# Front of a two-block kernel: modulation on TensorE in four column groups, all look-ups in one stretch, modulation tiles between the halves of a burst

## The chip, the core and the metric

One program runs on one core of a Trainium2 chip. The engines are TensorE (PE in the profile; its weight loads are PEld), VectorE (DVE), ScalarE (ACT), GpSimd (POOL), and SyncE (SP), whose queue issues the loads of weights. Each runs its own list of instructions in order and waits on semaphores. The metric is the time of one execution on the device, in microseconds (us), smaller is better.

## What is computed

Two blocks of a network on a sequence of 256 tokens and width 2048, in fp32. The change touches only the start of the first block:

```python
c_act = silu(c)
mod = c_act @ w_mod[l] + b_mod[l]                # (1, 2048) @ (2048, 6144)
shift, scale, gate = split(mod, 3)
h = rmsnorm(x, norm_gain[l]) * (1 + scale) + shift
proj = h @ w_in[l]                               # (256, 2048) @ (2048, 7248)
...
bias = rel_bias[t5_bucket(pos_q - pos_k)]        # table of 32 buckets x 8 heads
```

The rest (sparse attention, retention, output projection, a second layer, then a block with a convolution, a gated recurrence and a gated embedding) is computed as before.

## The kernel before

**Matmuls.** fp32 operands are split into a high and a low part: `w_hi` by ScalarE, `w_lo = raw - w_hi` by VectorE, and likewise `ht_hi`, `ht_lo` for the activations. A product is three matmuls (hi x hi, lo x hi, hi x lo), at L843 to L845 in the front and L684 to L686 in `gemm`. The output is made in chunks of 512 columns.

**The ring.** `raw` is a ring of four tiles of 1 MB (128 partitions x 4 x 512 fp32). SyncE loads tile t into place t % 4 when tile t-4 has been read. A tile of `w_in` holds four k-tiles of a chunk; it is split in two halves, each with a place in `w_hi` and `w_lo`, four places in all, which PE frees.

**The front** handles 40 tiles, in four rounds i = 0 to 3. Tiles 10i to 10i+7 are `w_mod`: the shift and scale columns of k-tiles 4i to 4i+3. Tiles 10i+8 and 10i+9 are the rows of `w_in` for these k-tiles, for the first two chunks. In a round:

- `modulate` (L2075, L2078), VectorE: multiplies each tile by the column of silu(c) and adds it up in `macc`, two instructions a tile; then one addition of the two halves (L2105).
- `pair_sums` (L816), PE: eight fp32 matmuls with a column of ones sum `macc` over the partitions, which puts shift and scale into columns.
- `columns` (L2062, L2065), VectorE: adds `b_mod`, and forms the scale with `norm_gain`.
- `turn_rows` (L828), PE, and `turned_rows` (L1377), ScalarE: transposes of the scaled rows of x.
- `formed_tiles` (L1393, L1395), ScalarE, and `tiles_low` (L2086), VectorE: apply scale and shift and split the result.
- `quarter_half(i, g, h)` (L843 to L845), PE: twelve matmuls with half h of the `w_in` tile of chunk g; four of them are the burst of a round.

**The look-ups** of the position bias, 24 steps, run between all this. A step: PE spreads the bucket numbers over partitions (`spread_keys`, L778, bf16); ScalarE makes a one-hot matrix by Abs and Relu (L1368, L1370, fp32); PE multiplies it with the table `rb_diag` (`look_up`, L790, four fp32 matmuls of 32 columns). Every four steps ScalarE copies the result to `bias` (`bias_out`). `STEPS` spreads the steps: four before round 0, one or two around each quarter of rounds 0 to 2.

PE runs an fp32 matmul as two instructions, so the trace counts eight for four.

## Time and profile before

| | |
|---|---|
| median of three runs | 1871.63 us (1869.8 to 1871.9) |
| the profiled execution | 1869.93 us, its span 1868.1 us |
| PE busy | 1826.4 us, 98% |
| VectorE, ScalarE busy | 1351.8 and 990.8 us, 72% and 53% |
| DMA, mean of the span | 227 GB/s |

The span is the time from the first to the last instruction of the profiled execution; the rest of its time lies around it. A matmul's end in the profile is modelled and overlaps the next, so the distance of starts is what a matmul costs. "Releaser" is the event that ended a wait.

### The profile page before, as it was taken

The page shows a single profiled execution, that of the slowest core. Times are in us where ns is not written, and L with a number is a line of the kernel's source. Part 1 is how long each engine was busy: PE and PEld are TensorE (multiplying, and loading weights), DVE is VectorE, ACT ScalarE, POOL GpSimd, SP SyncE. Part 2 cuts the span into 40 slices and gives each one's busy share as a digit, 9 for nine tenths or more (in the row PEclk, how much of TensorE's full clock was granted, in tenths as well). Part 3 has the DMA queues.
Part 4 walks back from the last instruction along what each step waited for, and adds up shares of the span by engine and source line. Part 5 has one row for each costly group of instructions (what it writes and reads, how often), then busy time and mean ns, then how long its engine had stood idle before and what let it go on. Part 6 is the DMA issues. An engine that isn't in the chain of part 4 may idle for free.

```text
span 1868.1 us, 25006 instructions
## 1 busy us (share of the span) xinstructions
PE 1826.4 (98%) x9520; PEld 1512.4 (81%) x9520; DVE 1351.8 (72%) x1949; ACT 990.8 (53%) x1359; POOL 203.0 (11%) x256
## 2 busy tenths in 40 slices
PE   5989999999999999999999999999999999999997
PEld 3768788889888878888888888888888888888886
DVE  6979999988987778857765544488885466665555
ACT  6664455446447445544654644476765445444464
POOL 0000002100000000210000000044441020031001
PEclk9989999999999999999999999999999999999999
DMA  9989978965986986744365555554555555557562
GB/s 350 373 323 343 332 232 302 322 224 182 330 297 229 361 280 225 235 159 159 124 225 185 182 199 192 191 181 161 177 178 182 185 191 184 184 180 248 182 197 94
DMA packets 211826, 424.07 MB, mean 227 GB/s; under 512 B 7680, under 2 KB 12684, under 8 KB 210316
## 3 DMA queue, kind: packets, MB, share of 16 engines
q1 hardware_dynamic: 209788, 414.94, 65.6%
q10 hardware_dynamic: 1936, 7.76, 1.0%
q8 instruction: 66, 1.08, 0.2%
q14 instruction: 36, 0.29, 0.0%
HBM read 418.45 MB, written 4.21 MB: 226 GB/s over the span
## 4 chain that ended last, share of the span: by engine, by line
PE 91%; DMA 3%; DVE 2%; ACT 2%; issue 1%; SPq 0%; DVEq 0%; POOLq 0%; POOL 0%; ACTq 0%
PE acc L684 28%; PE acc L686 28%; PE acc L685 28%; DMA raw<-in_w_in 2%; DVE scr L2078 1%; DMA raw<-in_w_mod 1%; PE tps L725 1%; PE tps L765 1%; ACT w_hi L1418 0%; ACT proj L1393 0%; PE sps L996 0%; PE tps L988 0%; PE sps L952 0%; PE sps L893 0%; PE sps L892 0%
## 5 line engine op out<-in xcount | busy, mean ns | idle before, releaser
L1859 DVE TENSOR_TENSOR w_lo<-raw,w_hi 128x1024 fp32r<-128x1024 f32 (+1 forms) x580 | 721.1, 1249 | 444.8 <-ACT w_hi L1246 442.5
L1246 ACT ACTIVATE w_hi<-raw 128x1024 fp32r<-128x1024 f32 (+1 forms) x580 | 606.1, 1050 | 762.3 <-PE acc L686 684.3
L684 PE MATMUL acc<-w_hi,ht_hi 128*128 128x512 f32 (+1 forms) x2304 | 910.5, 395 | 0.5 <-issue 0.4
L686 PE MATMUL acc<-w_hi,ht_lo 128*128 128x512 f32 (+1 forms) x2304 | 894.2, 388 | 0.0
L685 PE MATMUL acc<-w_lo,ht_hi 128*128 128x512 f32 (+1 forms) x2304 | 892.3, 387 | 0.0
L686 PEld LDWEIGHTS acc<-w_hi,ht_lo 128*128 128x128 f32 x2304 | 432.4, 188 | 90.3
L684 PEld LDWEIGHTS acc<-w_hi,ht_hi 128*128 128x128 f32 x2304 | 432.9, 188 | 87.4 <-issue 3.2
L685 PEld LDWEIGHTS acc<-w_lo,ht_hi 128*128 128x128 f32 x2304 | 433.3, 188 | 83.4
L1989 DVE SCALAR_TENSOR_TENSOR scr<-raw,vcol,scr 128x512 f32<-128x512 f32 x154 | 110.9, 761 | 4.8 <-issue 0.4
L2078 DVE SCALAR_TENSOR_TENSOR scr<-raw,vcol,scr 128x1024 f32<-128x1024 f32 x56 | 68.0, 1278 | 6.6 <-DMA raw<-in_w_mod 6.6
L1989 DVE SCALAR_TENSOR_TENSOR proj<-raw,vcol,proj 128x512 f32<-128x512 f32 x70 | 52.3, 788 | 1.9
L2684 POOL TENSOR_TENSOR scr<-scr 128x128 f32<-128x128 f32 x56 | 31.0, 586 | 157.0 <-DVE scr L2433 157.0
L2621 POOL COPY xn<-proj 128x128 f32<-128x128 f32 x4 | 2.5, 652 | 330.8 <-ACT proj L1483 330.8
L2655 POOL TENSOR_TENSOR proj<-proj 128x512 f32<-128x512 f32 x8 | 13.4, 1688 | 223.9 <-ACT proj L1602 192.8
L843 PE MATMUL acc<-w_hi,ht_hi 128*128 128x512 f32 x64 | 29.7, 465 | 7.2 <-DVE ht_lo L2086 7.2
L790 PEld LDWEIGHTS sps<-proj 128*128 128x128 f32 x192 | 28.9, 230 | 6.8 <-ACT proj L1370 4.2
L790 PE MATMUL sps<-proj 128*128 128x32 f32 x192 | 30.3, 307 | 3.3 <-ACT scr L1357 1.6
L1466 ACT ACTIVATE proj<-acc,st 128x512 f32<-128x512 f32 (+1 forms) x50 | 31.4, 679 | 0.1
L2646 POOL TENSOR_TENSOR scr<-scr,proj 128x384 f32<-128x384 f32 x16 | 23.2, 1447 | 56.2 <-DVE st L2248 56.2
L2720 POOL TENSOR_TENSOR xn<-proj 128x256 f32 x16 | 19.5, 1236 | 79.3 <-DVE proj L2528 48.6
L1483 ACT ACTIVATE proj<-acc 128x1024 f32<-128x1024 f32 (+1 forms) x26 | 25.7, 988 | 4.4 <-PE acc L845 4.3
L844 PE MATMUL acc<-w_lo,ht_hi 128*128 128x512 f32 x64 | 27.8, 434 | 0.0
(305 smaller groups left out, 1446.8 us busy)
## 6 DMA issues: line engine op xcount, KB each, us to landing
raw<-in_w_in SPq DMA_DIRECT2D x208, 1024.0 KB, 5.1
raw<-in_w_mod SPq DMA_DIRECT2D x64, 1024.0 KB, 6.2
raw<-in_w_mod SPq DMA_DIRECT2D x64, 512.0 KB, 6.3
raw<-in_w_out SPq DMA_DIRECT2D x32, 1024.0 KB, 5.2
raw<-in_w_o SPq DMA_DIRECT2D x16, 1024.0 KB, 5.2
raw<-in_w_ple_gate SPq DMA_DIRECT2D x16, 1024.0 KB, 5.1
raw<-in_w_b_out SPq DMA_DIRECT2D x8, 1024.0 KB, 5.1
raw<-in_w_a_out SPq DMA_DIRECT2D x8, 1024.0 KB, 5.1
```

The lines of the kernel that those rows point to most:

```text
L684: pe.matmul(o, hi_m, w_hi[:, slot, u, 0:width], start=start, stop=False)
L685: pe.matmul(o, hi_m, w_lo[:, slot, u, 0:width], start=False, stop=False)
L686: mm = pe.matmul(o, lo_m, w_hi[:, slot, u, 0:width], start=False, stop=stop)
L790: mm = pe.matmul(bias_cols[:, c:c + KPG * NH], onehot[:, n % 2, e * w + m * P:e * w + (m + 1) * P], rb_diag, start=True, stop=True)
L843: pe.matmul(o, hi_m, w_hi[:, slot, u, :], start=kt == 0, stop=False)
L844: pe.matmul(o, hi_m, w_lo[:, slot, u, :], start=False, stop=False)
L1246: act.activation(w_hi[:, x % SPL, :, 0:width], raw[:, j, 2 * (x % halves):2 * (x % halves) + 2, 0:width], ACT.Copy).then_inc(hi_ready, 1)
L1466: r = act.activation(o[:, m, :], acc[:, b, m, :], func, scale=st[:, 22 + m:23 + m])
L1859: dve.tensor_tensor(w_lo[:, x % SPL, :, 0:width], raw[:, j, 2 * (x % halves):2 * (x % halves) + 2, 0:width], w_hi[:, x % SPL, :, 0:width]. ...
L1989: r = dve.scalar_tensor_tensor(to[:, e, :], raw[:, slot, 2 * u + e, :], v2("c", kt), to[:, e, :], ALU.mult, ALU.add)
L2078: r = dve.scalar_tensor_tensor(to, src, v2("c", kt), to, ALU.mult, ALU.add)
L2684: pool.tensor_tensor(first_half[0], mid, first_half[1], ALU.subtract)
```

## The change

Four things change in the front, and nothing behind it.

1. *Modulation on PE.* `mod_slot(i, j)` multiplies tile 10i+j: four fp32 matmuls of 512 columns. The stationary operand is a column of silu(c) repeated 32 times, so each matmul fills one group of 32 columns of the array and writes 32 partitions of one bank of PSUM (`tps`, half 1): k-tile parity and shift or scale give the group. VectorE copies the bank after the eighth tile (`rows_out`), and `pair_sums` becomes four matmuls of two columns with `picks`, which adds the two parities. The ring place of a `w_mod` tile is freed by PE (`mod_read`); SyncE's waits are counted by `slot_free(t)`.
2. *Look-ups in one stretch.* All 24 come before round 0's burst, with tiles 1 to 7 of round 0 between them (`MOD_AFTER`). The one-hot is one VectorE comparison to bf16; `rb_diag` is split into three bf16 parts by GpSimd, so a step has 12 bf16 matmuls. Key columns go through four banks of `acc`, results through two of `sps`.
3. *Slots between halves of a burst.* Tiles 0 and 1 of round i+1 come after the first quarter of burst i, 2 and 3 after the second, 4 to 7 after the third; then come `turn_rows`, `pair_sums` of round i+1, the fourth quarter, and the second `turn_rows`.
4. *ScalarE's order* follows: a round is `w_hi`, `formed_tiles`, `w_hi`, `formed_tiles`, `w_hi` twice, then `scaled_rows` and both `turned_rows` of the next round.

```diff
-FIRST_STEPS = 4
-STEPS = [(0, 1, (1, 1, 2, 1)), (1, 1, (1, 1, 2, 1)), (1, 1, (1, 1, 2, 1)), (0, 0, (0, 0, 0, 0))]
+MOD_AFTER = {0: 1, 2: 2, 6: 3, 9: 4, 12: 5, 16: 6, 20: 7}
...
+            def slot_free(t):
+
+                i, j = divmod(t - RAW, 10)
+                if t < RAW:
+                    return
+                if j < 8:
+                    sp.wait_ge(mod_read, 8 * i + j + 1)
+                else:
+                    sp.wait_ge(raw_read, 8 + 4 * i + 2 * (j - 7))
...
-                        mm = pe.matmul(bias_cols[:, c:c + KPG * NH], onehot[:, n % 2, e * w + m * P:e * w + (m + 1) * P],
-                                       rb_diag, start=True, stop=True)
+                        for b in range(3):
+                            mm = pe.matmul(bias_cols(n)[:, c:c + KPG * NH], onehot[:, n % 4, e * w + m * P:e * w + (m + 1) * P],
+                                           rb_parts[:, b, :], start=b == 0, stop=b == 2)
...
+            def mod_slot(i, j):
+
+                t = 10 * i + j
+                if j == 0:
+                    pe.wait_ge(mod_taken, 1 + 2 * i)
+                pe.wait_ge(raw_landed[t % RAW], landed_start(t))
+                for u in range(2):
+                    c_col = v2("c", 2 * j + u).broadcast_to([P, 32])
+                    for b in range(2):
+                        g = 32 * (2 * b + u)
+                        mm = pe.matmul(tps[g:g + 32, 1, :], c_col, raw[:, t % RAW, 2 * u + b, :], start=j == 0, stop=j == 7)
+                mm.then_inc(mod_read, 1)
...
-            for i, (a, b, inside) in enumerate(STEPS):
-                pair_sums()
-                steps(n, a + b)
-                n += a + b
-                lo.skip(16)
-                for q, (g, h) in enumerate(((0, 0), (0, 1), (1, 0), (1, 1))):
-                    quarter_half(i, g, h)
-                    steps(n, inside[q])
-                    n += inside[q]
-                    if i < 3 and q < 2:
-                        turn_rows(4 * (i + 1) + 2 * q)
+            pair_sums()
+            for i in range(4):
+                for q in range(4):
+                    quarter_half(i, q // 2, q % 2)
+                    if i < 3 and q < 3:
+                        mod_slots(i + 1, 2 * q, 4 if q == 2 else 2)
+                        if q == 2:
+                            turn_rows(4 * (i + 1))
+                            pair_sums()
+                if i < 3:
+                    turn_rows(4 * (i + 1) + 2)
...
             for i in range(4):
                 for g in range(2):
                     t = 10 * i + 8 + g
...
                         act.activation(w_hi[:, 2 * g + h, :, :], raw[:, t % RAW, 2 * h:2 * h + 2, :], ACT.Copy)\
                            .then_inc(hi_ready, 1)
+                        if g == 0:
+                            formed_tiles(4 * i + 2 * h)
+                if i < 2:
+                    scaled_rows(i + 2)
                 if i < 3:
+                    turned_rows(4 * (i + 1))
+                    turned_rows(4 * (i + 1) + 2)
...
+            def rows_out(i):
+
+                dve.wait_ge(mod_summed, m_free.next(2))
+                dve.wait_ge(mod_read, 8 * (i + 1))
+                dve.tensor_copy(mrows, tps[:, 1, :]).then_inc(mod_ready, 1)
...
+            for j in range(24):
+                dve.wait_ge(keys_spread, j + 1)
+                if j >= 4:
+                    dve.wait_ge(onehot_used, j - 3)
+                dve.tensor_scalar(onehot[:, j % 4, :], key_cols(j), kst[:, C_NB:C_NB + 1], 0.0, ALU.add, ALU.is_equal)\
+                   .then_inc(onehot_ready, 1)
```

On PE, in the program of before, the end of burst 0 and the sums of round 1 stand like this (L778 and L790 are a look-up step; the burst's repeated rows are left out at "..."):

```order
L843 MATMUL acc<-w_hi,ht_hi 128x512
L844 MATMUL acc<-w_lo,ht_hi 128x512
L845 MATMUL acc<-w_hi,ht_lo 128x512
L778 MATMUL sps<-proj 128x256 x2
L790 MATMUL sps<-proj 128x32 x4
L816 MATMUL tps<-kst,scr 128x1 x8
```

and in the changed program, from the third quarter of burst 0 on (L846 is `mod_slot`, L870 `turn_rows`, L859 `pair_sums`, L885 to L887 the quarters):

```order
L887 MATMUL acc<-w_hi,ht_lo 128x512
L846 MATMUL tps<-raw,vcol 32x512 x16
L870 MATMUL tps<-kst,proj 128x128 x4
L859 MATMUL tps<-kst,scr 128x2 x4
L885 MATMUL acc<-w_hi,ht_hi 128x512
...
L887 MATMUL acc<-w_hi,ht_lo 128x512
L870 MATMUL tps<-kst,proj 128x128 x4
```

Tiles 4 to 7 of the next round (16 matmuls) and its sums now stand ahead of the fourth quarter, and the second group of transposes behind it; in before the whole burst stood ahead of the next sums, and the transposes between its quarters.

On ScalarE in the changed program, from the `w_hi` of chunk 1 in round 0 to the first ones of round 1 (L1454 is `w_hi`, L1420 `scaled_rows`, L1413 `turned_rows`, L1428 and L1430 `formed_tiles`), with what each waits for:

```order
L1454 ACTIVATE w_hi<-raw 128x1024 [waits split_used]
L1420 ACTIVATE proj<-xres,st 128x512 x2
L1413 ACTIVATE proj<-tps 128x512 [waits xt_turned] x2
L1454 ACTIVATE w_hi<-raw 128x1024 [waits split_used,raw_landed2]
L1428 ACTIVATE proj<-proj,modc,acol 128x256 [waits columns_ready]
L1428 ACTIVATE proj<-proj,modc,acol 128x256
L1430 ACTIVATE ht_hi<-proj 128x512 [waits tiles_formed]
L1454 ACTIVATE w_hi<-raw 128x1024 [waits split_used]
```

Both transposed row tiles of the next round are copied ahead of its first `w_hi`, and forming stands between the two halves of a `w_in` tile. In before the copies stood between look-up steps, and the two `w_hi` of a tile side by side:

```order
L1377 ACTIVATE proj<-tps 128x512 [waits xt_turned]
L1368 ACTIVATE proj<-sps,kst 128x512 [waits onehot_used,keys_spread]
L1370 ACTIVATE proj<-proj,kst 128x512 [waits spread_read]
...
L1418 ACTIVATE w_hi<-raw 128x1024 [waits split_used,raw_landed2]
L1418 ACTIVATE w_hi<-raw 128x1024 [waits split_used]
```

On VectorE the start of the front is now, all look-ups ahead of round 0 (L2120 the comparison, L2104 the row copy, L2134 `w_lo`, L2110 `ht_lo`):

```order
L2120 TENSOR_SCALAR proj<-acc,kst 128x512 x16
L2000 TENSOR_TENSOR proj<-vcol 128x8
L2104 COPY scr<-tps 128x512
L2094 TENSOR_TENSOR modc<-tps,vcol 128x2x4
L2097 SCALAR_TENSOR_TENSOR acol<-modc,vcol 128x4
L2134 TENSOR_TENSOR w_lo<-raw,w_hi 128x1024
```

The 64 products of `modulate` that stood there and in every round are gone.

## Rows read from the trace of the kernel before

**Rows 1.** The page's chain that ended last, shares of the span by engine.
```profile
PE 91%; DMA 3%; DVE 2%; ACT 2%; issue 1%; SPq 0%; DVEq 0%; POOLq 0%; POOL 0%; ACTq 0%
```

**Rows 2.** Stretches: length; PE, PEld, DVE, ACT, POOL busy; PEclk, DMA share, GB/s.
```profile
20.00:50.00 30.00, 21.60 (x85) 17.71 (x86) 26.02 (x28) 23.49 (x42) 0.00 (x0) 1.00 1.05 387
80.00:110.00 30.00, 27.38 (x167) 22.99 (x167) 27.22 (x27) 20.30 (x32) 0.00 (x0) 0.89 1.01 366
```

**Rows 3.** Chain of waits in order of time: start, length, what.
```profile
31.42 8.48 DMA raw<-in_w_in
...
116.44 8.63 DMA raw<-in_w_in
...
130.38 0.79 PE acc L843
```

**Rows 4.** Timeline: start, length, instruction, [idle before, releaser]; third and last burst.
```profile
118.73 0.48 PE L843 MATMUL acc<-w_hi,ht_hi 128*128 128x512 f32 x1
...
119.30 2.48 DVE L2078 SCALAR_TENSOR_TENSOR scr<-raw,vcol,scr 128x1024 f32<-128x1024 f32 x2 [0.49 <-DMA raw<-in_w_mod]
...
121.33 0.39 PE L845 MATMUL acc<-w_hi,ht_lo 128*128 128x512 f32 x1
...
123.19 1.92 PE L816 MATMUL tps<-kst,scr 128*128 128x1 f32 x16 [0.65 <-DVE scr L2105]
...
130.97 0.63 PE L844 MATMUL acc<-w_lo,ht_hi 128*128 128x512 f32 x1
...
133.51 0.40 PE L844 MATMUL acc<-w_lo,ht_hi 128*128 128x512 f32 x1
```

**Rows 5.** Groups by line, 0 to 143 us: busy, mean ns | idle before, releaser.
```profile
L2078 DVE SCALAR_TENSOR_TENSOR scr<-raw,vcol,scr 128x1024 f32<-128x1024 f32 x56 | 68.0, 1278 | 6.6 <-DMA raw<-in_w_mod 6.6
...
L790 PEld LDWEIGHTS sps<-proj 128*128 128x128 f32 x192 | 28.9, 230 | 6.8 <-ACT proj L1370 4.2 <-ACT scr L1357 2.4
...
L2113 DVE TENSOR_TENSOR w_lo<-raw,w_hi 128x1024 fp32r<-128x1024 f32 x16 | 19.2, 1222 | 3.2 <-ACT w_hi L1418 3.1
L1370 ACT ACTIVATE proj<-proj,kst 128x512 f32<-128x512 f32 x24 | 17.4, 723 | 0.8
...
L1418 ACT ACTIVATE w_hi<-raw 128x1024 fp32r<-128x1024 f32 x16 | 16.0, 1047 | 8.5 <-DMA raw<-in_w_in 8.5
...
L1393 ACT ACTIVATE proj<-proj,modc,acol 128x256 f32<-128x256 f32 x16 | 8.6, 588 | 0.6 <-DVE acol L2065 0.6
...
L1395 ACT ACTIVATE ht_hi<-proj 128x512 fp32r<-128x512 f32 x8 | 5.0, 630 | 0.7
...
L1377 ACT ACTIVATE proj<-tps 128x512 f32<-128x512 f32 x8 | 4.8, 598 | 19.4 <-PE tps L828 19.4
...
L778 PEld LDWEIGHTS sps<-proj 128*128 128x128 bf16 x64 | 4.2, 106 | 12.9 <-ACT proj L1368 8.4 <-issue 3.1 <-DVE proj L1963 1.1
```

**Rows 6.** Timeline of PE at fp32 matmuls elsewhere in the kernel.
```profile
297.62 0.60 PE L952 MATMUL sps<-proj,scr 128*128 128x256 f32 x2
298.05 0.38 PE L951 MATMUL sps<-proj,scr 128*128 128x128 f32 x2
...
1247.41 0.73 PE L1078 MATMUL sps<-scr 128*32 128x32 f32 x62
...
1247.96 0.20 PE L1078 MATMUL sps<-scr 128*32 128x32 f32 x1
```

**Rows 7.** Timeline: first spread, one fp32 look-up, four transposes.
```profile
17.70 0.61 PE L778 MATMUL sps<-proj 128*128 128x256 bf16 x2 [0.73 <-DVE proj L1963]
...
43.85 1.92 PE L790 MATMUL sps<-proj 128*128 128x32 f32 x8 [0.69 <-ACT scr L1357]
...
52.65 0.64 PE L828 MATMUL tps<-kst,proj 128*128 128x128 f32 x4
```

**Rows 8.** Groups by line and shape on DVE: a read of 384 PSUM columns.
```profile
L1963 DVE SCALAR_TENSOR_TENSOR proj<-sps,proj 128x384 bf16<-128x384 f32 x1 | 0.6, 558 | 2.7 <-PE sps L797 2.7
```

**Rows 9.** The page's DMA issues: count, size, us from issue to landing.
```profile
raw<-in_w_in SPq DMA_DIRECT2D x208, 1024.0 KB, 5.1
```

More of the change, by code:

```diff
@@ L69 @@
 C_PW = C_HPI + 1
-C_TH = C_PW + 2
+C_SEL = C_PW + 2
+C_TH = C_SEL + 2
 C_N = C_TH + NB - EXACT - 1
@@ L528, in _ @@
             free = Seen(sp, raw_read)
+            def slot_free(t):
[6 more added lines that the diff above has]
+                    sp.wait_ge(raw_read, 8 + 4 * i + 2 * (j - 7))
             def mod_pair(i, j):
                 slot = (10 * i + j) % RAW
-                sp.wait_ge(raw_read, free.next(2))
+                slot_free(10 * i + j)
                 for b in range(2):
@@ L570, in _ @@
                 for g in range(2):
-                    land((10 * i + 8 + g) % RAW, full(wi[0])(i, CHUNKS[g] * CH, CH))
+                    slot_free(10 * i + 8 + g)
+                    slot = (10 * i + 8 + g) % RAW
+                    sp.dma_start(raw[:, slot, :, :], full(wi[0])(i, CHUNKS[g] * CH, CH)).then_inc(raw_landed[slot], 16)
+            free.skip(16)
             for l in range(DEPTH):
@@ L777, in spread_keys @@
                     at = P * (g0 + e)
-                    mm = pe.matmul(key_cols[:, e * w:(e + 1) * w], key_pick[:, at:at + P], b_t, start=True, stop=True)
+                    mm = pe.matmul(key_cols(n)[:, e * w:(e + 1) * w], key_pick[:, at:at + P], b_t, start=True, stop=True)
                 mm.then_inc(keys_spread, 1)
             def look_up(n):
-                if n % 4 == 0 and n:
-                    pe.wait_ge(bias_ready, n // 4)
+                if n % 4 == 0 and n >= 8:
+                    pe.wait_ge(bias_ready, n // 4 - 1)
                 pe.wait_ge(onehot_ready, n + 1)
@@ L799, in _, with mod_slots @@
             pe.wait_ge(buckets_ready, 1)
-            pe.wait_ge(s_rb, 16 * KPG)
+            pe.wait_ge(rb_split, 1)
             spread_keys(0)
-            def steps(n, count):
-                for j in range(n, n + count):
-                    if j < 23:
-                        spread_keys(j + 1)
-                    look_up(j)
+            spread_keys(1)
+            pe.wait_ge(vec_ready, 1)
+            def mod_slot(i, j):
[9 more added lines that the diff above has]
+                mm.then_inc(mod_read, 1)
+            def mod_slots(i, first, count):
+                if i < 4:
+                    for j in range(first, first + count):
+                        mod_slot(i, j)
             def pair_sums():
-                pe.wait_ge(mod_taken, m_taken.next())
-                m_taken.skip(1)
+                m_taken.skip(2)
                 pe.wait_ge(mod_ready, m_ready.next())
-                for b in range(2):
-                    for j in range(4):
-                        mm = pe.matmul(tps[:, 1, 4 * b + j:4 * b + j + 1], macc[:, b, 0, j * P:(j + 1) * P], ones,
-                                       start=True, stop=True)
+                for j in range(4):
+                    mm = pe.matmul(tps[:, 1, 2 * j:2 * j + 2], mrows[:, j * P:(j + 1) * P], picks, start=True, stop=True)
                 mm.then_inc(mod_summed, 2)
@@ L1360, in bias_out @@
                 r.then_inc(bias_ready, 1)
-            def steps(n, count):
-                for j in range(n, n + count):
-                    o = onehot[:, j % 2, :]
-                    act.wait_ge(keys_spread, j + 1)
-                    if j >= 2:
-                        act.wait_ge(onehot_used, j - 1)
-                    act.activation(o, key_cols, ACT.Abs, bias=kst[:, C_NB:C_NB + 1]).then_inc(spread_read, 1)
-                    act.wait_ge(spread_read, j + 1)
-                    act.activation(o, o, ACT.Relu, bias=ones, scale=-1.0).then_inc(onehot_ready, 1)
-                    if j % 4 == 0 and j:
-                        bias_out(j // 4 - 1)
             def turned_rows(k):
@@ L1406, in _ @@
             act.activation(vcol[:, P + KT:P + NV2], tps[:, 0, P + KT:P + NV2], ACT.Copy).then_inc(vec_ready, 1)
+            bias_out(3)
             turned_rows(0)
+            bias_out(4)
+            scaled_rows(1)
             turned_rows(2)
-            for i, (a, b, inside) in enumerate(STEPS):
+            bias_out(5)
+            for i in range(4):
                 for g in range(2):
                     t = 10 * i + 8 + g
-                    if g:
-                        steps(n, a)
                     for h in range(2):
@@ L2115, in _ @@
                         own.skip(1)
-                for e in range(2):
-                    if i < 3:
-                        if e == 0:
-                            dve.wait_ge(mod_summed, m_free.next(2))
-                        modulate(i + 1, 0, e)
-                    tiles_low(4 * i + 2 * e)
+                        if g == 0:
+                            tiles_low(4 * i + 2 * h)
             results.skip(16)
```

136 lines of the change are left out of this document (64 added, 72 removed).

## The prediction

> **What bounds the kernel now.** I read the chain that ended last first. Its line by engine [rows 1] gives 91% of the span to the matrix engine (PE), so a change that neither removes matmul time nor moves a stretch in which PE waits can do nothing. The table by stretches [rows 2] then says where PE waits: in the front the DMA engines are busy at 1.01 to 1.05 of their time and move 366 to 387 GB/s, while PE has holes, and its granted clock averages 0.89 from 80 to 110 us. The chain of waits in time [rows 3] joins the two: tiles of `w_in` land at 39.90 and 125.07 us (start plus length of the DMA rows), ScalarE and VectorE split the last and form `ht`, and at 130.38 PE starts the last round's burst of matmuls for the first two chunks. From there the chain is PE's. So the front is a stream of 40 tiles of 1 MB, and everything behind it is PE's. What moves the start at 130.38 moves the end by as much, and only that counts here.
>
> How fast can the stream go? At 387 GB/s a tile of 1.049 MB takes 2.71 us; call it 2.7. From tile 9 (39.90) to tile 39 (125.07) 30 tiles took 85.2 us, which is 81.0 at that rate and 4.2 us lost. Tile 37, the last of `w_mod`, landed at 119.30 [rows 4], where VectorE's wait for it ends. Hence a perfect stream gains about 4 us, 0.2%, and that is the ceiling of this change unless it shortens what comes behind the last tile.
>
> **What the change removes.** On VectorE the 56 multiply-adds of 1.28 us and 8 first products [rows 5], and on ScalarE an Abs and a Relu for each of 24 look-ups, the Relu 0.72 us [rows 5]. Neither engine ends the front except where it holds a tile of the ring of four. In before a `w_mod` tile is held for 2.5 us, within the 2.7 of the next transfer. So the removal is hidden under the DMA, and would come out on the path only as part of those 4.2 us.
>
> **What PE gets.** A tile of `w_mod` is now four fp32 matmuls over 512 columns. The trace shows fp32 over 256 columns as two instructions in 0.43 us (297.62 to the next at 298.05) [rows 6], so 512 columns cost 0.86 us at the higher clock and 1.7 at the lower. Do the four 32-column groups run at once? The nearest row is 62 fp32 instructions of 32x32 into different groups, whose starts fill 0.73 less one duration of 0.20, 0.53 us, 8.6 ns each [rows 6], where 32 of 256 columns' worth would be 27 ns: three at a time. I take 0.9 to 1.0 us a tile. The page "TensorE: Matmul & The Clock Gate" of the Trainium skill (Part 3) has a measured 2.38x for three column groups over 512 columns; by that a tile would be about 1.1 us by estimate, and the sum would grow by some 0.2 us a round.
>
> A look-up step keeps its two bf16 spreads and has 12 bf16 matmuls of 32 columns for 8 fp32 instructions. The latter took 1.92 us at the lower clock [rows 7] and are paced by their weight loads, 230 ns mean; bf16 loads are 106 ns [rows 5]. So 12 cost between 0.4 and 1.3 us at the lower clock; I take 0.6, with 0.43 for the spreads: 1.0 a step, 0.5 at the higher clock. VectorE's comparison reads 512 columns of PSUM: 384 took 0.56 [rows 8], so in proportion at most 0.74 and not under 0.56; I take 0.69, or 0.75 with the hand-off. VectorE sets the pace of a step where the clock is high, PE where it is low.
>
> **First stretch.** Look-ups start as before at 17.70 [rows 7]. 24 steps of 0.75 are 18 us, and seven tiles of 0.9 between them 6.3: about 42 us. Before, two thirds of the look-ups lay later, under the DMA stream. What is queued behind them now? ScalarE issues all six copies of the bias before the first `w_hi`, and VectorE all 24 comparisons before the first row copy. So tile 8, which landed in before at 37.2 (2.7 ahead of tile 9), waits: row copy 0.65, sums 0.96, forming 1.81, second `w_hi` 1.05, second `w_lo` 1.22 (all priced below), hand-offs and two small operations 0.9 give 48.6 us for its release. A transfer on an idle queue takes 5.1 us from issue to landing [rows 9], 2.4 more than its 2.7, so tile 12 flows from 51.0. The stream, if full, is done with tile 11 at 39.90 + 2 x 2.7 = 45.3. Idle 5.7 us.
>
> **Rounds 1 and 2.** This is the term on which the forecast rests, and the order of instructions shows it. PE's burst of round i is stretched over the whole round: its fourth quarter comes only after the eighth modulation tile and the sums of round i+1. ScalarE must turn the last two row tiles, which PE transposes after that quarter, before it may touch the first `w_in` tile of round i+1, although that tile landed long ago. The tile's place in the ring is thus late. Counted from the landing of the last `w_mod` tile, at the higher clock: PE multiplies it, 1.0; VectorE copies rows, 0.65; sums, half of the 16 instructions in 1.92 us [rows 4], 0.96; a quarter, 12 matmuls, eleven starts in 2.60 us [rows 4], 2.8; transposes 0.64 [rows 7]; ScalarE's copy 0.60, `w_hi` 1.05, forming 1.81 (two of 0.59 and one of 0.63), `w_hi` 1.05; VectorE's `w_lo` 1.22 [rows 5]; hand-offs 0.7. That is 12.5 us, and with 2.4 to the first byte 14.9. Four tiles, the rest of the ring, cover 10.8. Idle 4.1 us. The second `w_in` tile is released 4.0 us after the first (forming and two `w_hi` more), the transfer covers 2.7: 1.3 more. Each such round loses 5.4 us.
>
> In before the burst of a round ran beside the multiply-adds: the fourth quarter of round 2 had its last matmul at 121.33, two us behind the landing of tile 37 [rows 4], so nothing held the first `w_in` tile.
>
> **The sum.** Losses: first stretch 5.7 + 1.3 = 7.0; two rounds (tiles 22 and 32) 10.8; together 17.8 us. If all of the 4.2 us lost in before disappear, tile 37 is 13.6 us later, if none 17.8; I take the middle, 15.7. Behind tile 37 the way to PE's last burst is the same chain up to forming, 1.0 + 0.65 + 0.96 + 2.8 + 0.64 + 0.60 + 1.05 + 1.81 + 0.7 + 0.6 = 10.8 us, against 130.38 - 119.30 = 11.1 before. No term. The profiled execution took 1869.9 us (span 1868.1 and 1.8 around it), 1.7 below the median of the three runs: 1869.9 + 15.7 = 1885.6, on the median's scale 1887.
>
> **The rivals.**
> *The clock stays low.* In before the last burst begins with matmuls 0.63 us long, at 130.97, and has 0.40 at 133.51 [rows 4], the lower and the higher level; a stretch of the front averages 0.89 [rows 2]. If PE keeps the lower level (1.2 GHz of 2.4) in the look-ups, 24 steps of 1.0 and eight tiles of 1.8 take 38.4 instead of 24 us, 14 more; in each of two rounds the tile, the sums, a quarter and the transposes cost 0.85 + 0.95 + 2.4 + 0.4, 4.6 more. Up to 23 us on top, 1910; half of it 1899. For it: new rounds have a tile of 1 us and then 1.7 of nothing. Against: tiles are dense matmuls and the first stretch is full of work. By "TensorE: Matmul & The Clock Gate" of the Trainium skill, a DMA wait between all matmuls makes PE run cold; the trace agrees in that its clock fell where PE waited. Chance 0.26.
> *The groups don't run together.* With the two instructions of a matmul blocking the next group, 1.7 us a tile: 7 us in the first stretch, 0.9 a round, about 1896; all serial, 3.4 us a tile exceeds the transfer, and eight tiles and a burst of 11 make a round of 40 us against 27, over 1930. Against it are [rows 6]. 0.07.
> *Faster: the ring never runs dry.* If the chain of 12.5 us is under 8.4 (10.8 less 2.4), the stream is full, tile 37 lands at 39.90 + 28 x 2.7 = 115.5 instead of 119.30, and the time is 3.8 us lower, 1868. It is decided at the release of the first `w_in` tile of a round. The first stretch would have to be done by 35 us too, which VectorE's 18 us alone from 17.70 nearly forbid. 0.09.
> *No difference*: half of the chain is shorter than I count and the 4.2 us come back against the rest. 0.05; a loss of 4 to 8 us, 0.03.
> My case has 0.50, with a range of its own of 1881 to 1894.
>
> **The numbers.** A measurement here tells 0.2%, 3.7 us, from no change. Faster 0.09, same 0.05, slower 0.86. The range leaves out the faster case and the top of the low-clock and serial cases: 1873 to 1909.
>
> **What would show it.** Right: in the changed profile DMA share under 0.9 in three places, about 46 to 51, and twice some 30 us later each; rounds of about 32 us where they are 28 now (30 tiles in 85.2); ScalarE's first `w_hi` of a round waiting for PE's transposes, not for a landing; PE's last burst of the front starting at about 146. The modulation tile at 0.9 to 1.0 us, starts of four groups together. Wrong: first `w_hi` right after a landing and DMA share above 1.0 to the end of the front (faster), or 0.43 us a matmul in most bursts (slower still). A look-up step far from 0.75 us moves the first term alone.

## The result: 1.1% slower

| | before | changed |
|---|---|---|
| median | 1870.72 us (1868.33 to 1871.9, 4 runs) | 1890.49 us (1886.81 to 1893.64, 4 runs) |
| ratio | | 1.0107 (95%: 1.0084 to 1.0129) |
| profiled execution, its span | 1869.93, 1868.1 us | 1886.81, 1884.7 us |
| last burst of the front starts | 130.38 | 147.03 |
| VectorE, ScalarE busy | 1351.8, 990.8 us | 1294.4, 959.3 us |

The forecast was 1887 with a range from 1873 to 1909. VectorE and ScalarE are relieved of 57 and 32 us of work, and the program is 20 us slower. In the profiled executions all of the difference, 16.6 us of span, is there when the last burst begins (147.03 - 130.38 = 16.65).

### The profile page after: what moved, and what is told of

Same layout as the page of the kernel before. It is cut to its first block, busy times and chain, and to the rows that moved or that the text cites. A ratio compares the mean times of both kernels' runs of the same rounds, so it can differ in the third digit from the quotient of the medians.

```text
span 1884.7 us, 25534 instructions
## 1 busy us (share of the span) xinstructions
PE 1838.9 (98%) x9840; PEld 1496.3 (79%) x9840; DVE 1294.4 (69%) x1909; ACT 959.3 (51%) x1311; POOL 203.9 (11%) x261
## 4 chain that ended last, share of the span: by engine, by line
PE 95%; DMA 2%; DVE 1%; ACT 1%; issue 1%; SPq 0%; ACTq 0%; DVEq 0%; POOLq 0%; POOL 0%
PE acc L714 28%; PE acc L716 27%; PE acc L715 27%; DMA raw<-in_w_mod 2%; PE tps L846 1%; PE tps L755 1%; PE acc L885 1%; PE acc L886 1%; PE tps L795 1%; PE acc L887 1%; PE sps L828 0%; PE sps L941 0%; PE acc L808 0%; PE sps L1044 0%; PE tps L1036 0%
## 5 line engine op out<-in xcount | busy, mean ns | idle before, releaser
L714 PEld LDWEIGHTS acc<-w_hi,ht_hi 128*128 128x128 f32 x2304 | 432.8, 188 | 87.4 <-issue 2.9
L846 PE MATMUL tps<-raw,vcol 128*32 128x512 f32 x256 | 36.7, 662 | 9.9 <-DMA raw<-in_w_mod 9.9
L885 PE MATMUL acc<-w_hi,ht_hi 128*128 128x512 f32 x64 | 30.3, 473 | 15.5 <-DVE ht_lo L2110 15.5
L1413 ACT ACTIVATE proj<-tps 128x512 f32<-128x512 f32 x8 | 4.8, 597 | 76.4 <-PE tps L870 76.4
L2104 DVE COPY scr<-tps 128x512 f32<-128x512 f32 x4 | 2.8, 690 | 54.8 <-PE tps L846 54.8
L885 PEld LDWEIGHTS acc<-w_hi,ht_hi 128*128 128x128 f32 x64 | 14.2, 222 | 24.2 <-DVE ht_lo L2110 16.3
L2134 DVE TENSOR_TENSOR w_lo<-raw,w_hi 128x1024 fp32r<-128x1024 f32 x16 | 19.2, 1224 | 16.3 <-ACT w_hi L1454 16.2
```

What stands on the lines that cost most here:

```text
L714: pe.matmul(o, hi_m, w_hi[:, slot, u, 0:width], start=start, stop=False)
L846: mm = pe.matmul(tps[g:g + 32, 1, :], c_col, raw[:, t % RAW, 2 * u + b, :], start=j == 0, stop=j == 7)
L885: pe.matmul(o, hi_m, w_hi[:, slot, u, :], start=kt == 0, stop=False)
```

## The profile after

The chain of the changed kernel by engine, and stretches of it (start:end, length, busy us and instructions of PE, PEld, DVE, ACT and POOL, then PEclk, DMA share, GB/s). They answer to [rows 1] and [rows 2]:

```profile
PE 95%; DMA 2%; DVE 1%; ACT 1%; issue 1%; SPq 0%; ACTq 0%; DVEq 0%; POOLq 0%; POOL 0%
```

```profile
20.00:50.00 30.00, 26.59 (x434) 18.10 (x431) 20.90 (x33) 18.05 (x37) 0.00 (x0) 0.93 0.88 313
44.00:54.00 10.00, 7.39 (x28) 4.24 (x28) 6.17 (x6) 7.35 (x11) 0.00 (x0) 0.66 0.54 173
54.00:76.00 22.00, 17.00 (x104) 9.37 (x100) 1.02 (x3) 1.96 (x3) 0.00 (x0) 1.00 1.04 383
76.00:88.00 12.00, 9.28 (x40) 5.79 (x40) 6.20 (x6) 7.46 (x12) 0.00 (x0) 0.86 0.69 230
80.00:110.00 30.00, 23.67 (x125) 12.43 (x123) 4.91 (x8) 6.57 (x10) 0.00 (x0) 0.89 0.97 347
88.00:108.00 20.00, 15.67 (x89) 7.70 (x88) 1.02 (x3) 0.93 (x2) 0.00 (x0) 0.91 1.05 388
108.00:122.00 14.00, 10.24 (x44) 6.39 (x44) 6.20 (x6) 7.27 (x11) 0.00 (x0) 0.76 0.67 221
```

A full stream has a DMA share of 1.04 to 1.05 here and moves 383 to 388 GB/s. The shares of 0.54, 0.69 and 0.67 mark three holes, one a round; between them the stream is full. How long a hole is I read from the landings, as the forecast did: a tile is late by what it lands more than 2.7 us behind its predecessor. Tiles 12 and 13 are 5.3 us late together, 22 and 23 4.9, 32 and 33 6.1, 16.4 us in all. The bytes in the rows above say the same (387 - 173 of 387 GB/s over 10 us is 5.5, then 4.9 and 6.0); the share of busy time alone would give 4.9, 4.1 and 5.1, which is too little. VectorE, busy for 27 of 30 us in [rows 2], now works for 1.0 us in the 20 from 88 to 108: what the change set free had not bounded these rounds. (The PEclk of 1.00 in the first line of [rows 2] is not the level of the first burst of before: its matmuls start 0.43 us apart from 46.34 us on, the lower level, as they do in the changed kernel from 46.61.)

Why the hole opens is in the chain of waits of round 1 (start, length, what; the quarter's twelve matmuls are cut to two):

```profile
59.53 8.71 DMA raw<-in_w_mod
...
68.28 1.11 PE tps L846 x8
...
69.48 0.70 DVE scr L2104
...
70.23 1.05 PE tps L859 x8
71.29 0.34 PE acc L885
...
73.93 0.23 PE acc L887
74.16 0.45 PE tps L870 x4
...
75.13 1.05 ACT w_hi L1454
76.17 0.99 ACT proj L1428 x2
```

Tile 17, the last of `w_mod`, lands at 68.24. The `w_in` tile behind it lands at 70.95 and is then left alone: ScalarE takes it up at 75.13, when PE has gone through the tile, the sums, a whole quarter and the transposes. VectorE's second `w_lo` from it ends at 80.08, and only then may the place be loaded again.

The last round, in the timeline:

```profile
133.50 1.94 PE L846 MATMUL tps<-raw,vcol 128*32 128x512 f32 x8 [0.79 <-DMA raw<-in_w_mod]
135.36 1.12 PE L870 MATMUL tps<-kst,proj 128*128 128x128 f32 x4
...
136.31 1.87 PE L859 MATMUL tps<-kst,scr 128*128 128x2 f32 x8
...
139.04 0.63 PE L887 MATMUL acc<-w_hi,ht_lo 128*128 128x512 f32 x1
...
142.94 0.60 ACT L1413 ACTIVATE proj<-tps 128x512 f32<-128x512 f32 x1 [5.83 <-PE tps L870]
143.43 1.05 ACT L1454 ACTIVATE w_hi<-raw 128x1024 fp32r<-128x1024 f32 x1
...
147.03 0.50 PE L885 MATMUL acc<-w_hi,ht_hi 128*128 128x512 f32 x1 [4.13 <-DVE ht_lo L2110]
```

Here PE runs at its lower level: the row of the tile is 1.94 us long where it was 1.11 at 68.28, the matmuls of the quarter start 0.43 us apart and not 0.23. From the start of tile 7's multiplication to the first matmul of the burst it is 10.44 us in round 1 (78.72 - 68.28) and 13.53 in the last.

## The experiments

All are edits of the changed kernel and compute what it computes. A tile is "late" by what it lands more than 2.7 us behind its predecessor; the middle columns add this up for the two tiles that follow each pair of `w_in` tiles in the ring. The last two columns are the start of the last burst and how long that is after the landing of tile 37, the last of `w_mod`. All but the ratio are of the one profiled execution.

| run | ratio to before (95%) | 12, 13 late | 22, 23 late | 32, 33 late | last burst at | behind tile 37 |
|---|---|---|---|---|---|---|
| before | 1 | 0 | 0 | 0 | 130.4 | 11.1 |
| the changed kernel | 1.0107 (1.0084 to 1.0129) | 5.3 | 4.9 | 6.1 | 147.0 | 13.6 |
| early_turn | 1.0054 (1.0040 to 1.0068) | 7.3 | 4.8 | 3.0 | 140.8 | 7.7 |
| slots_two | 1.0015 (1.0006 to 1.0024) | 6.0 | 2.8 | 1.0 | 133.6 | 6.3 |
| late_look | 1.0098 (1.0082 to 1.0113) | 4.1 | 8.6 | 9.1 | 154.6 | 13.5 |
| both | 1.0022 (1.0013 to 1.0031) | 3.3 | 4.7 | 2.0 | 135.2 | 6.3 |
| warm | 1.0090 (1.0074 to 1.0107) | 6.5 | 7.5 | 6.0 | 150.3 | 11.7 |
| warm_few | 1.0080 (1.0066 to 1.0094) | 6.5 | 5.6 | 4.2 | 146.1 | 10.5 |
| two_groups | 1.0134 (1.0117 to 1.0151) | 6.1 | 5.7 | 5.7 | 153.5 | 11.3 |
| whole_burst | 1.0155 (1.0138 to 1.0172) | 6.6 | 2.6 | 2.5 | 159.4 | 7.9 |
| hi_first | 1.0009 (1.0000 to 1.0018) | 3.0 | 0 | 0.7 | 131.5 | 7.3 |
| tuned | 0.9987 (0.9978 to 0.9996) | 1.5 | 0.9 | 0 | 129.2 | 7.3 |
| after_again (no edit) | 1.0111 (1.0094 to 1.0128) | 5.4 | 8.6 | 10.5 | 155.1 | 14.4 |

**early_turn: the second transposes ahead of the fourth quarter.**

```diff
                             pair_sums()
-                if i < 3:
-                    turn_rows(4 * (i + 1) + 2)
+                            turn_rows(4 * (i + 1) + 2)
```

> The changed kernel with the second group of row transposes of the next round moved on TensorE from behind the fourth quarter to ahead of it. Order theory (ScalarE's first w_hi of a round waits for the copy of these transposes, and they for the quarter): in the changed kernel's profile the quarter takes 2.85 us at 71.15 and ScalarE's w_hi starts at 75.13; it should start some 2.8 us earlier, the idle time of the DMA stream ahead of tiles 22 and 32 should fall from 3.7 and 4.5 us to about 1 and 1.5, and the last burst, which starts at 147.03, should start about 9 us earlier, near 138: some 9 us less than the changed kernel, 1.006 of before (now 1.0107). Clock theory (what is lost comes from TensorE at its lower level): the order of two small groups changes no clock, so under 2 us less. First-stretch theory (the 5 us lost ahead of tile 12 are most of it and the rest is fixed): under 3 us less.

Half of the loss went with one moved line: 1.0107 to 1.0054, 9.9 us by the ratios. In round 1 ScalarE's `w_hi` now starts at 75.54 for a tile taken up at 70.46, 5.1 us behind, where it was 6.85 (75.13 - 68.28), although PE was at its lower level:

```profile
75.05 0.60 ACT L1412 ACTIVATE proj<-tps 128x512 f32<-128x512 f32 x1 [0.97 <-PE tps L870]
75.54 1.05 ACT L1453 ACTIVATE w_hi<-raw 128x1024 fp32r<-128x1024 f32 x1
```

The lateness of tiles 22 and 32 fell from 3.7 and 4.6 us to 2.6 and 0.4, that of 23 and 33 rose from 1.2 and 1.6 to 2.2 and 2.6: the second `w_in` tile, behind both formings, is the next limit. The last burst started at 140.8 and not at the forecast 138, 6.3 us earlier than in the changed kernel, and 5.9 of these 6.3 us lie behind tile 37 (7.7 us for 13.6), where the changed kernel also ran at the lower level, which cost it 3.1 us (above). So the order is worth some 2.8 us there. In rounds 1 and 2 the holes fell from 11.0 to 7.8 us together, but the first stretch, which the edit does not touch, lost 2.0 us more in this execution. How the 9.9 us divide between order and clock this run does not tell.

**slots_two: two modulation tiles behind every quarter.**

```diff
-                    if i < 3 and q < 3:
-                        mod_slots(i + 1, 2 * q, 4 if q == 2 else 2)
-                        if q == 2:
-                            turn_rows(4 * (i + 1))
-                            pair_sums()
+                    if i < 3:
+                        mod_slots(i + 1, 2 * q, 2)
+                        if q in (1, 2):
+                            turn_rows(4 * (i + 1) + 2 * (q - 1))
                 if i < 3:
-                    turn_rows(4 * (i + 1) + 2)
+                    pair_sums()
```

> The changed kernel with two modulation tiles behind each of the four quarters in place of two, two, four and none, both groups of row transposes behind the second and third quarter, and the sums last. Order theory: no quarter stands any more between the last w_mod tile and the first w_hi. From that landing the chain is tile 1.0, row copy 0.7, sums 1.0, two small operations 0.4, forming, w_hi and w_lo, about 7.8 us to the release of the first w_in tile, under the 8.4 (four tiles of 2.7 less 2.4) that a full stream allows. Idle ahead of tiles 22 and 32 about 0, ahead of 23 and 33 about 0.6: 9 to 10 us less up to tile 37 (133.5 in the changed kernel), and 5 to 6 less behind it, since the last burst then starts 7.5 us behind tile 37 and not 13.5. Last burst near 131.5, time about that of before, 0.999 to 1.002 of it. Clock theory: the waits for tiles are as long as before, the clock falls as often, and no more than 5 us come back, 1.008. First-stretch theory: under 3 us.

1.0015, 17 us less than the changed kernel; the first `w_hi` of a round waits for its own transfer:

```profile
65.57 0.60 ACT L1412 ACTIVATE proj<-tps 128x512 f32<-128x512 f32 x1 [4.83 <-PE tps L870]
72.00 1.06 ACT L1453 ACTIVATE w_hi<-raw 128x1024 fp32r<-128x1024 f32 x1 [5.83 <-DMA raw<-in_w_in]
```

```profile
44.00:54.00 10.00, 6.83 (x32) 4.13 (x32) 6.53 (x8) 8.17 (x12) 0.00 (x0) 0.83 0.56 183
...
76.00:88.00 12.00, 10.98 (x48) 6.22 (x47) 4.01 (x4) 4.44 (x7) 0.00 (x0) 0.78 0.96 335
...
108.00:122.00 14.00, 13.26 (x79) 6.93 (x82) 2.38 (x3) 1.72 (x3) 0.00 (x0) 0.98 0.94 337
```

The second and third hole shrink to 2.8 and 1.0 us, while the first, which the edit doesn't touch, stays (6.0 us, 5.3 before the edit). The clock fell here too (0.78 from 76 to 88), so it cannot be the main cause of what was lost. The last burst, forecast near 131.5, starts at 133.6.

**late_look and both: eight look-ups moved into round 0.** In `late_look` 16 look-ups stand first; the others follow one by one behind quarters and tiles of round 0, with their columns in the two banks of `sps`. `both` has this and `slots_two`.

```diff
+            def look_on(i, n):
+                if i == 0:
+                    look_up(n)
+                    if n < 23:
+                        spread_keys(n + 1)
...
```

> The changed kernel with 16 look-ups ahead of the first burst and the last eight one by one behind quarters and modulation tiles of round 0 (keys and results in the two banks of sps, as in before). Order theory with its first term: the first stretch ends some 6 us earlier, the release of tile 8 with it, so that the idle time of 4.3 us ahead of tile 12 and 1.0 ahead of tile 13 goes; the later rounds keep theirs (3.7 and 4.5 us). Last burst 147.0 less 5 = 142, time 5 us less, 1.008 of before. If the look-ups are not what holds tile 8 (the clock or the sums do), 0 to 1 us less. If eight steps in the round delay the modulation tiles, up to 3 us come back.

> The two edits together (two modulation tiles behind each quarter, and 16 look-ups first with eight in round 0). Order theory: the stream is never dry; tile 37 lands at 38 + 29 x 2.7 = about 117.5 to 118 with small losses, the last burst starts 7.5 behind it, at 125 to 126, where before has 130.38: 4 to 5 us faster than before, 0.9975. If the two gains overlap, or a low clock is the cost, 1.000 to 1.005.

Neither came as expected. `late_look` is not told from the changed kernel (1.0098, intervals overlap), `both` not from `slots_two`. The first burst did start earlier, at 43.8 and 44.4 where it was 46.6 and 47.4. But the look-ups were not gone, only moved into a round that has no room on PE. In `both`, from 50 to 72 us:

```profile
50.00:72.00 22.00, 21.79 (x232) 12.46 (x224) 5.50 (x9) 2.96 (x5) 0.00 (x0) 0.99 0.97 349
```

```profile
69.34 1.06 PE L851 MATMUL tps<-raw,vcol 128*32 128x512 f32 x8
69.44 0.75 DVE L2139 TENSOR_SCALAR proj<-sps,kst 128x512 bf16<-128x512 f32 x1 [2.98 <-PE sps L813]
70.33 0.47 PE L826 MATMUL sps<-proj 128*128 128x32 bf16 x12
...
70.73 1.06 PE L851 MATMUL tps<-raw,vcol 128*32 128x512 f32 x8
```

PE is busy for 21.8 of 22 us, and no tile of the round's end (L851) waits for a transfer: tile 17 landed at 67.17 and is multiplied at 70.73, so PE is late. In `late_look` tiles 12 and 13 are 1.2 us less late than in the changed kernel, but tile 17 is 1.5 us late itself and lands at 68.60, where it was 68.24: what the shorter first stretch won was gone by then. The larger holes behind it cannot be put down to the edit. The profiled execution of `late_look` was the slowest of its four (1894.4 us, two others 1886.2 and 1886.5), all three of its fourth quarters ran at the lower level, and `after_again`, without any edit, shows holes as large. My forecast had priced the first stretch, not what its work costs elsewhere.

**warm and warm_few: TensorE kept busy in its waits.** bf16 matmuls that nothing reads, eight (`warm`) or three (`warm_few`) behind each of the tiles 4 to 6, and sixteen behind the last transposes of a round. As they write the banks that held the look-ups' results, the first burst also waits for the last copy of the bias (`bias_ready`) in both runs; it started no later for it (46.6 and 46.1).

```diff
+            def fill(n):
+                for k in range(n):
+                    pe.matmul(sps[:, k % 2, 0:384], ident_b, key_pick[:, 0:384], start=True, stop=True)
...
```

> The changed kernel with work added that nothing reads: eight bf16 matmuls of 384 columns behind each of the modulation tiles 4, 5 and 6 of a round, and sixteen behind the last transposes of a round, into the two banks of sps, free by then. They fill TensorE's waits for transfers and for the forming. Clock theory (rival of the forecast): if waiting is what lets the granted clock fall, these stretches stay at the higher level, tiles at 133.5 take 1.0 and not 1.94, the quarter behind them 2.85 and not 4.3, the last burst's first 8 matmuls 0.23 and not 0.43 each: about 4 to 6 us less than the changed kernel, 1.008 of before. Order theory alone: these low stretches are a cost of 1 us in a round and 2.5 at the end, so 3 to 4 us less at most, and the DMA stream stays idle ahead of tiles 22 and 32. If the added matmuls only lengthen the chain: 0 to 3 us more.

> The changed kernel with three added matmuls of 384 columns behind the modulation tiles 4, 5 and 6 in place of the eight of the run warm (sixteen behind the last transposes as there). In warm the clock stayed at the higher level from the fourth quarter to the last burst, and from the start of tile 7's multiplication to the burst it was 10.45 us against 13.5 in the last round of the changed kernel, but the eight matmuls kept tile 7 waiting for some 2 us a round. Clock theory: with 0.6 us of filling the tile is not late, and the clock stays high where the filling is: 3 to 6 us less than the changed kernel, 1.008 of before. If three are too few to keep the clock: like the changed kernel, 1.0105.

With three, the last round of the front reads:

```profile
135.64 1.06 PE L846 MATMUL tps<-raw,vcol 128*32 128x512 f32 x8 [1.72 <-DMA raw<-in_w_mod]
...
137.59 1.05 PE L868 MATMUL tps<-kst,scr 128*128 128x2 f32 x8 [0.29 <-DVE scr L2115]
...
141.81 2.77 PE L852 MATMUL sps<-proj 128*128 128x384 bf16 x16
146.11 0.50 PE L894 MATMUL acc<-w_hi,ht_hi 128*128 128x512 f32 x1 [1.54 <-DVE ht_lo L2121]
```

```profile
134.00:138.00 4.00, 2.07 (x16) 0.99 (x16) 0.69 (x1) 0.60 (x1) 0.00 (x0) 1.00 1.05 386
138.00:142.00 4.00, 4.00 (x24) 3.40 (x24) 0.33 (x2) 0.00 (x0) 0.00 (x0) 1.00 1.05 387
142.00:146.00 4.00, 2.57 (x16) 1.98 (x14) 1.86 (x2) 3.90 (x6) 0.00 (x0) 1.00 0.50 185
146.00:150.00 4.00, 3.89 (x17) 3.23 (x18) 3.07 (x4) 3.89 (x7) 0.00 (x0) 1.00 0.29 75
```

The clock is 1.00 to the burst and through it, and tile to burst takes 10.47 us again, so the 13.53 of the changed kernel are 10.5 of work and 3.1 of lower clock. The time is 5.0 us under that of the changed kernel (1.0080 for 1.0107; 1.0111 in its second comparison, below), with intervals that just overlap. Three quarters of the loss stayed, so the clock is the smaller part of it. The 5.0 us are net: what the fillers themselves cost is in them too. With eight the clock was 1.00 from the fourth quarter to the last burst as well (the third quarters, from 94.05 and 128.06, still ran 0.43 us apart), and the time was 1.0090, not told from the changed kernel: at 139.88 tile 37 was multiplied 1.2 us after it had landed (138.7), because the fillers stood ahead of it.

**two_groups: four column groups against two.**

```diff
-                        g = 32 * (2 * b + u)
+                        g = 32 * (2 * b + j % 2)
```

(with `start` for the first and `stop` for the last matmul of each group).

> The changed kernel with the four matmuls of a modulation tile in two column groups (the tile's parity picks which two of the four, so the sums are the same) and not in four. In the changed kernel a tile takes 0.99 us at the higher clock where four matmuls one by one would be 3.4. If the overlap comes from the groups, a tile takes 1.75 us, 0.75 more; the first stretch holds eight of them between the look-ups (5 to 6 us longer), a round's chain one (0.8, twice, and once at the end): 7 to 8 us more than the changed kernel, 1.015 of before. If the matmuls overlap whatever group they are in, or the tile is hidden by the transfers everywhere: 0 to 1 us more.

```profile
75.61 1.91 PE L846 MATMUL tps<-raw,vcol 128*32 128x512 f32 x8 [0.80 <-DMA raw<-in_w_mod]
77.45 0.66 PE L871 MATMUL tps<-kst,proj 128*128 128x128 f32 x4
```

A tile takes 1.84 us (77.45 - 75.61) with two groups and 1.00 with four (69.28, where the transposes start, less 68.28), at the same clock. The overlap comes from the groups, and is nearly complete: four matmuls one by one would be 3.4. The time is 1.0134, 5.0 us more than the changed kernel by the ratios, with intervals that overlap. The profile is clearer: with eight such tiles ahead of it the first burst starts at 53.9, and in the two executions of the changed kernel at 46.6 and 46.2.

**whole_burst: no slots inside a burst.** Four quarters in a row, then the transposes, the eight tiles, the sums.

> The changed kernel with the slots taken out of the burst: four quarters in a row, then both groups of transposes, then the eight modulation tiles and the sums. Order theory: the quarter is no longer in the chain behind the last w_mod tile (5 us less per round there, 5 to 6 at the end), but the next round's first two tiles wait for 11 us of burst in the ring in place of 5, so that some 5 us of the stream are lost at the ring's other end in each of three rounds. About even with the changed kernel: 5 less to 5 more, 1.008 to 1.013. If slots inside the burst are themselves what costs (more waits, a lower clock): 8 us less or better. If the ring is what matters and the fourth quarter is not: 10 to 15 more.

1.0155, 9.0 us more than the changed kernel, so more than the 5 that I gave as the most, and short of the 10 to 15 for "the ring is what matters":

```profile
54.00:76.00 22.00, 16.48 (x91) 7.13 (x89) 0.00 (x0) 1.19 (x2) 0.00 (x0) 0.81 0.69 243
...
88.00:108.00 20.00, 16.05 (x89) 9.49 (x88) 1.73 (x2) 2.71 (x5) 0.00 (x0) 0.93 0.61 209
```

The ring fills with `w_mod` while PE is in the burst: tiles 14, 24 and 34 are late by 7.2, 7.7 and 8.1 us, new idle time at another place. Where the quarter has left the chain, the holes do shrink (2.6 and 2.5 us for 4.9 and 6.1), as does the way behind tile 37 (7.9 us, at the lower level). So the slots themselves are right; what costs is the quarter that is left behind the last of them.

**hi_first and tuned: the order mended at both ends.** `hi_first` is `slots_two` with ScalarE in the order of `w_hi` twice, forming, `w_hi` twice, forming. `tuned` also splits tile 8 ahead of the second row copy and the last bias copy, tile 9 ahead of the forming, and has PE multiply tiles 0 and 1 of round 1 ahead of the first burst; its look-ups are all first, as in the changed kernel.

```diff
+            high_halves(0, 0)
             turned_rows(2)
             bias_out(5)
+            high_halves(0, 1)
+            formed_tiles(0)
+            formed_tiles(2)
+            scaled_rows(1)
...
```

> The kernel of two tiles behind each quarter (slots_two, 1.0015 of before), with both w_hi of the first w_in tile ahead of the forming on ScalarE, both w_hi of the second ahead of the second forming (in the last round both formings stand together), and VectorE's w_lo and ht_lo to match. In slots_two's profile the stream is idle for 4.5 us ahead of tile 12, 1.5 ahead of 13, 2.9 ahead of 23 and 1.1 ahead of 32. Order theory: the first w_in tile is released 1.8 us earlier and the second 1.8 us earlier (the second forming is behind it), so about 1.8 of the 6.0 in the first stretch and 2 to 3 of the 4.0 later come back: 3.5 to 4.5 us less than slots_two, 0.9992 to 1.0 of before. If what is left comes from the burst reaching the next round's slots late (TensorE's work and clock, not ScalarE's order): 0 to 1.5 us less, 1.001.

> hi_first with the first stretch reordered too: all 24 look-ups stay first, but ScalarE splits tile 8 ahead of its second row copy and last bias copy, and tile 9 ahead of the forming, VectorE's first w_lo stands ahead of the row copy, and TensorE multiplies the first two tiles of round 1 ahead of the first burst, so that the fourth quarter of round 0 comes last. Order theory: the idle 4.5 + 1.5 us ahead of tiles 12 and 13 fall to under 1.5, tile 37 lands near 118 to 120, the last burst starts near 127: 3 to 5 us faster than before, 0.9975 to 0.9985. If TensorE (8 us of tiles, 11 to 13 of burst and 3 of small work in a round of 27) or a lower clock has become the bound of the first round: 0.9995 to 1.001.

`hi_first` is 1.1 us below `slots_two`, where 3.5 to 4.5 were forecast, and their intervals overlap; it is not told from before either. `tuned` takes 0.9987 of before (0.9978 to 0.9996, 11 runs), 1.6 us less by the medians and 2.4 by the ratio, and is the fastest of all kernels here. The interval excludes 1, though the step is smaller than the 0.2% up to which I had called a result the same, and smaller than forecast (0.9975 to 0.9985, tile 37 by 120; it landed at 121.90).

```profile
44.00:54.00 10.00, 8.66 (x45) 4.16 (x45) 4.93 (x8) 7.18 (x12) 0.00 (x0) 0.83 0.92 315
...
124.63 2.00 ACT L1456 ACTIVATE w_hi<-raw 128x1024 fp32r<-128x1024 f32 x2 [6.15 <-DMA raw<-in_w_in]
...
125.05 0.17 DVE L2110 TENSOR_TENSOR modc<-tps,vcol 128x8 f32<-128x8 f32 x1 [1.22 <-PE tps L859]
...
129.19 0.80 PE L885 MATMUL acc<-w_hi,ht_hi 128*128 128x512 f32 x1 [4.25 <-DVE ht_lo L2126]
```

Where does `tuned` gain? Not in the stream: tiles 12 and 13 are still 1.5 us late, and tile 37 lands at 121.90, 2.6 us later than in before (119.27). It gains behind tile 37, 7.3 us to the burst where before has 11.1. Two things differ there. In before VectorE's last products (2.48 us at 119.30, [rows 4]) and an addition of 1.22 us stand ahead of PE's sums, which end 5.8 us behind the tile, and 3.0 us behind it in `tuned`. And in before VectorE forms the columns of shift and scale (`modc`) only behind its `w_lo` of tile 39, which waits for that tile's landing at 125.07:

```profile
126.18 1.23 DVE L2113 TENSOR_TENSOR w_lo<-raw,w_hi 128x1024 fp32r<-128x1024 f32 x1 [0.35 <-ACT w_hi L1418]
```

```profile
127.33 0.17 DVE modc L2062
```

The changed kernel and all its edits form them right behind the sums, in `tuned` at 125.05. No run tells the two apart. So the four parts of the change can be had without a loss, and the 0.1% is won behind the last tile, not out of the 4 us that a full stream could give.

**after_again: the changed kernel once more.**

> The changed kernel itself once more. Its profiled execution above took 1886.8 us, the other three 1889 to 1893.6, and only one of its three fourth quarters ran at the lower clock (starts 0.43 us apart, round 2's at 138.0). In the run late_look all three did, and each cost some 3 us more between the last w_mod tile and the next burst (13.3 against 10.45). If the spread of the times is this clock, an execution of 1889 to 1893 shows two or three fourth quarters or tiles before them at the lower level, and one that takes 1887 shows one. If the spread comes from elsewhere, the last burst starts at 147 whatever the time.

This execution took 1896.0 us, 9.2 more than the one above. Its fourth quarter in round 1:

```profile
103.41 1.93 PE L846 MATMUL tps<-raw,vcol 128*32 128x512 f32 x8 [1.65 <-DMA raw<-in_w_mod]
...
106.23 1.86 PE L859 MATMUL tps<-kst,scr 128*128 128x2 f32 x8
107.95 0.77 PE L885 MATMUL acc<-w_hi,ht_hi 128*128 128x512 f32 x1
109.38 0.63 PE L885 MATMUL acc<-w_hi,ht_hi 128*128 128x512 f32 x1
...
117.69 0.80 PE L885 MATMUL acc<-w_hi,ht_hi 128*128 128x512 f32 x1 [4.13 <-DVE ht_lo L2110]
```

All three fourth quarters ran at the lower level; tile to burst is 14.3 us here and 14.4 in the last round. The lower clock lengthens the chain in which the ring waits, so the holes of rounds 1 and 2 grow from 4.9 and 6.1 to 8.6 and 10.5 us. The last burst starts at 155.1 and not at 147.0, 8.1 of the 9.2 us. The other executions of the changed kernel fit: the mean granted clock is 0.989 in those of 1886.8 and 1888.3 us, 0.986 to 0.988 in those of 1889.0 to 1893.7, and 0.985 in this one. So the scatter of 7 us, where before scatters by 3.6, goes with how many stretches get the lower level. It also means that the profile shown first, the fastest of its four, shows less of the clock's cost than the median holds.

## Why the prediction was right, step by step

- *The bound.* Right: the start of the last burst carries the whole difference, 16.65 of 16.6 us. VectorE's 57 us bought nothing in the rounds. What they and VectorE's new order could buy lies behind tile 37, at most the 3.8 us of `tuned` (11.1 - 7.3); in the changed kernel a quarter stands in that place.
- *Rounds 1 and 2.* The step on which the forecast rested held. The chain from the last `w_mod` landing to the release of the first `w_in` tile was put at 12.5 us, at the higher clock. It is 11.8 in round 1 (68.24 to 80.08) and 12.9 in round 2 (100.18 to 113.12), where the modulation tile ran at the lower level; the second release, put 4.0 behind, is 3.8 behind. The holes were put at 5.4 each and are 4.9 and 6.1. `early_turn` and `slots_two` show the cause: without the quarter in the chain they are 2.8 and 1.0 in `slots_two`.
- *First stretch.* The hole was put at 7.0 and is 5.3. The look-ups ended where forecast (42 us) and tile 8 was released at 47.96, forecast 48.6. But the stream itself was not full ahead of it: tile 11 landed at 46.4 and not at 45.3, so the hole began later. The comparison takes 0.745 us in the trace, 0.69 to 0.75 in the forecast.
- *The sum.* Tile 37 landed at 133.45 (124.54 + 8.91), 14.15 later than in [rows 4], forecast 15.7. The forecast had 13.6 if all that before loses in its stream disappears and 17.8 if none, and took the middle; the measured value stands near the first. (Up to tile 37 before had lost 3.8 us, not the 4.2 that count to tile 39, so the first is 14.0.)
- *Behind tile 37.* "No term" was wrong: 13.6 us and not 10.8, where before has 11.1. That is the rival of the low clock, which I had held apart with 0.26; it does not replace the main case but comes on top of it. In the profiled execution it cost 3.1 us at the end. In the second one it cost some 3 to 4 in every round, which is near the 4.6 that the rival had for a round. `warm_few` gets back 5 us in the mean, fillers included.
- *The total* was closer than its terms. The profiled execution took 1886.8 us, forecast 1885.6: 1.5 us too much in the stream and 2.5 us left out behind it cancel in part, and that part is luck. The median is 1890.5, forecast 1887, because the other executions hold more of the lower clock.
- *Column groups.* 0.9 to 1.0 us a tile was forecast, 1.00 at the higher clock measured, 1.9 at the lower. The serial rival falls with `two_groups`.
- *The ring never runs dry* was put at 0.09. No order here shows it: in `tuned`, the nearest, tile 37 lands at 121.90 where the rival had 115.5, and its 0.9987 is won behind tile 37. The prediction called 4 us the ceiling "unless it shortens what comes behind the last tile"; that is how `tuned` gains.

The page "TensorE: Matmul & The Clock Gate" of the Trainium skill (Part 3) gives 2.38x for three column groups. In proportion four groups would give 3.2x, by estimate. Here four give 3.4x (3.4 us one by one, itself an estimate from [rows 6], against 1.00 measured), a little more.

Open: what decides in a given execution whether a fourth quarter runs at 1.2 or 2.4 GHz. The rows before it are alike in both executions (a wait of 1.65 us for the tile, a multiplication of 1.06, a wait of 1.65); one fourth quarter then ran 0.23 us a matmul, the other 0.43. Open too is how much of the loss is order and how much clock in the median: the runs bound the clock by about a quarter (`warm_few`), no closer. Not tried was a kernel in which only the waits inside the look-ups change.

## What to carry to other kernels

This ring was bound by its slowest release, not by the busiest engine. Before work is moved from one engine to another, follow each tile from landing to release through the *order* of every queue it passes: here one group of transposes behind a quarter cost 10 us by the ratios, and the 57 us that VectorE was spared gained nothing. When a stall at one end is mended by moving work, look for room where it goes (`late_look`, `both`), and spread what must be consumed at the pace of a stream so that nothing long stands behind the last piece (`slots_two`). When one program's executions differ, compare two of them before a hole is put down to an edit (`after_again`).

## What was not expected of the hardware

- fp32 matmuls in four column groups of TensorE run beside each other almost completely: 1.00 us for four of 512 columns, 1.84 in two groups, at the higher level; [rows 6] had shown three at a time.
- Added matmuls in the waits (`warm_few`) did not slow the kernel: three behind each of three tiles and sixteen behind the transposes kept the granted clock at 1.00 in the last round, where it had been 0.79 from 118 to 142 us, and the time was, if anything, shorter (1.0080 for 1.0107).
- Two profiled executions of one program differ by 9.2 us, with the same order and the same waits ahead of the fourth quarter of round 1: one had one fourth quarter at the lower level, the other three.
